# Decay and beta columns: the low parts of the weights beside the high ones in one weight tile

## The reference

```python
hn = rmsnorm(h, norm1)
proj = hn @ w_in                      # ga and gb are 8 columns each
beta = jax.nn.sigmoid(gb)
log_g = -jnp.exp(a_log) * jax.nn.softplus(ga + dt_bias)
o_a = gated_delta_chunked(gq, gk, gv, log_g, beta)
```

## Time and profile before

| | |
|---|---|
| median of three runs | 2068.93 us (2068.31 to 2069.67) |
| profiled execution | 2070.8 us |
| its span | 2069.0 us |
| TensorE busy | 2034.7 us (98%), 12940 matmul instructions |
| TensorE weight loads | 1949.7 us (94%) |
| VectorE busy | 1176.3 us (57%) |
| ScalarE busy | 626.6 us (30%) |
| GpSimd busy | 287.4 us (14%) |

### The profile page before, as it was taken

The page is one execution under the profiler, slowest core; times in us unless marked ns, Lnnn a source line. Parts: engine busy times, 40 slices in busy tenths (PEclk is TensorE's granted clock), DMA queues, the critical chain, the costliest instruction groups (busy, mean ns, idle before and its releaser), DMA issues.

```text
span 2069.0 us, 30409 instructions
## 1 busy us (share of the span) xinstructions
PE 2034.7 (98%) x12940; PEld 1949.7 (94%) x12940; DVE 1176.3 (57%) x1357; ACT 626.6 (30%) x794; POOL 287.4 (14%) x275
## 2 busy tenths in 40 slices
PE   8999999999999999999999999999999999999998
PEld 8999998999999999999999999999999999999996
DVE  6457565566667656566433343466565656565656
ACT  5223334434333444344443332211111111111113
POOL 0000003758370222222000002000000000000002
PEclk9999999999999999999999999999999999999999
DMA  9235666654555754645153221111011101110102
GB/s 281 93 103 136 142 158 202 187 191 154 163 154 133 173 177 137 187 146 156 60 186 109 88 70 51 62 61 52 31 51 51 52 31 51 52 53 31 60 31 82
DMA packets 252204, 227.11 MB, mean 110 GB/s; under 512 B 141102, under 2 KB 209622, under 8 KB 251942
## 3 DMA queue, kind: packets, MB, share of 16 engines
q1 hardware_dynamic: 252070, 225.17, 36.0%
HBM read 161.29 MB, written 63.84 MB: 109 GB/s over the span
## 4 chain that ended last, share of the span: by engine, by line
PE 91%; DVE 3%; ACT 2%; DMA 2%; issue 2%; SPq 1%; POOL 0%; POOLq 0%; DVEq 0%; ACTq 0%
PE a_psum L895 33%; PE a_psum L145 31%; PE a_psum L1164 11%; PE a_psum L882 5%; PE a_psum L970 1%; PE a_psum L988 1%; PE a_psum L1071 1%; PE a_psum L998 1%; PE a_psum L952 1%; PE a_psum L1014 1%; DMA w_raw<-in_w_in 1%; PE a_psum L967 1%; PE a_psum L1086 1%; PE a_psum L1094 1%; PE a_psum L1085 1%
## 5 line engine op out<-in xcount | busy, mean ns | idle before, releaser
L895 PE MATMUL a_psum<-xh,w_hi 128*128 128x342 f32 (+3 forms) x1656 | 535.6, 323 | 3.9 <-DVE w_lo L1515 3.9
L895 PE MATMUL a_psum<-xl,w_hi 128*128 128x342 f32 (+3 forms) x1656 | 531.4, 321 | 0.0
L895 PE MATMUL a_psum<-xh,w_lo 128*128 128x342 f32 (+3 forms) x1656 | 529.7, 320 | 0.0
L895 PEld LDWEIGHTS a_psum<-xh,w_hi 128*128 128x128 f32 x1656 | 312.2, 189 | 7.1 <-DVE w_lo L1515 4.5
L895 PEld LDWEIGHTS a_psum<-xl,w_hi 128*128 128x128 f32 x1656 | 312.3, 189 | 1.0
L895 PEld LDWEIGHTS a_psum<-xh,w_lo 128*128 128x128 f32 x1656 | 312.2, 189 | 0.0
L1218 ACT ACTIVATE w_hi<-w_raw 128x1024 fp32r<-128x1024 f32 x125 | 132.0, 1056 | 433.1 <-PE a_psum L145 409.5
L1293 ACT ACTIVATE post<-a_psum 128x342 f32<-128x342 f32 (+3 forms) x207 | 94.7, 457 | 554.2 <-PE a_psum L895 518.5
L145 PE MATMUL a_psum<-xh,w_hi 128*128 128x342 f32 (+1 forms) x1152 | 245.1, 321 | 9.2 <-DVE xl L1537 9.2
L1515 DVE TENSOR_TENSOR w_lo<-w_raw,w_hi 128x1024 fp32r<-128x1024 f32 x125 | 156.6, 1253 | 159.6 <-ACT w_hi L1218 159.6
L145 PE MATMUL a_psum<-xl,w_hi 128*128 128x342 f32 (+1 forms) x1152 | 245.1, 321 | 0.0
(11 more groups left out here) (239 smaller groups left out, 2807.8 us busy)
## 6 DMA issues: line engine op xcount, KB each, us to landing
w_raw<-in_w_in SPq DMA_DIRECT2D x76, 512.0 KB, 3.7
w_raw<-in_w_up SPq DMA_DIRECT2D x44, 512.0 KB, 3.5
mix_scratch<-post SPq DMA_DIRECT2D x32, 522.0 KB, 2.8
down_raw<-in_w_ffn_down SPq DMA_DIRECT2D x22, 512.0 KB, 4.3
ext<-mix_scratch SPq DMA_DIRECT2D x9, 1024.0 KB, 6.9
y<-mix_scratch SPq DMA_DIRECT2D x18, 512.0 KB, 5.5
ext<-grow_scratch SPq DMA_DIRECT2D x9, 512.0 KB, 5.5
ext<-mix_scratch SPq DMA_DIRECT2D x9, 512.0 KB, 6.8
```

The costliest lines, as they stand in the source:

```text
L895: mm = pe.matmul(psum[:, u % 2, 0:n], w[:, k, :], x[:, k, at0:at0 + n], start=(k == 0 and part == 0), stop=(k == KC - 1 and part == 2))
```

## The change

Tile 16 uses 16 of its 128 weight columns. After the change VectorE writes the low parts of these 16 columns not into the tile of low parts but into columns 16 to 31 of the tile of high parts. One product of x with the first 32 columns then gives both the high and the low weights' share, in rows 0 to 15 and 16 to 31 of PSUM. It is taken with x high and x low: 8 blocks x 2 x 3 thirds = 48 matmuls, with 32 weight columns each. (The share of low by low, which was left out before, is in it.) ScalarE copies 32 rows instead of 16 to `abT`. The turn is no longer nine transposes but nine ordinary float32 matmuls: `abT`'s 32 rows x 128 columns are the weights, and the moving operand is a new constant (`C_FOLD`) of 32 rows x 16 columns with ones where row modulo 16 is the column, so that a high and a low row are added as they are turned. The constants' table grows by 16 columns, which moves what lies behind it in SBUF by 64 bytes a partition.

```diff
+C_FOLD = C_BLK + 4
+C_W_ALL = C_FOLD + 2 * GH
...
+    c[:, C_FOLD:C_FOLD + 2 * GH] = i[:, None] % (2 * GH) == np.arange(2 * GH)[None, :]
...
-        abT = y[0:2 * GH, 0:2, :].rearrange("p k t -> p (k t)")[:, 0:TW]
+        abT = y[0:4 * GH, 0:2, :].rearrange("p k t -> p (k t)")[:, 0:TW]
...
                         if t == T_AB:
                             pe.wait_ge(x_split, KC + k + 1)
-                        mm = project_block(pe, psum, 2 + 3 * (t - T_AB + 1), wh[t % 2], wl[t % 2], xh, xl, k, 0, N3)
+                            for part, x in enumerate((xh, xl)):
+                                for j in range(3):
+                                    mm = pe.matmul(psum[0:4 * GH, 5 + j, 0:N3], wh[t % 2][:, k, 0:4 * GH],
+                                                   x[:, k, N3 * j:N3 * j + N3], start=(k == 0 and part == 0),
+                                                   stop=(k == KC - 1 and part == 1))
+                            continue
+                        mm = project_block(pe, psum, 2, wh[t % 2], wl[t % 2], xh, xl, k, 0, N3)
...
-                            mm = pe.transpose(psum[:, 7, c * 2 * GH:(c + 1) * 2 * GH],
-                                              abT[:, c * CH:c * CH + CH], ident[0:2 * GH, 0:2 * GH])
+                            mm = pe.matmul(psum[:, 7, c * 2 * GH:(c + 1) * 2 * GH], abT[:, c * CH:c * CH + CH],
+                                           const(C_FOLD, 2 * GH)[0:4 * GH, :], start=True, stop=True)
...
-                        act.activation(abT[:, LEAD:TW].rearrange("p (b c) -> p b c", b=3), psum[0:2 * GH, 5:8, 0:N3],
+                        act.activation(abT[:, LEAD:TW].rearrange("p (b c) -> p b c", b=3), psum[0:4 * GH, 5:8, 0:N3],
...
-                dve.tensor_tensor(lo, wr(t), hi.bitcast(F32), ALU.subtract).then_inc(w_lo, 1)
+                raw_w = wr(t)
+                if t == T_AB:
+                    n = 2 * GH
+                    hi, lo, raw_w = hi[:, :, 0:n], hi[:, :, n:2 * n], raw_w[:, :, 0:n]
+                dve.tensor_tensor(lo, raw_w, hi.bitcast(F32), ALU.subtract).then_inc(w_lo, 1)
```

More of the change, by code:

```diff
@@ L84 @@
 C_BLK = C_RCOL + RH
-C_W_ALL = C_BLK + 4
+C_FOLD = C_BLK + 4
+C_W_ALL = C_FOLD + 2 * GH
 RV_STEPS = ([(0, 512, (c,)) for c in range(9)]
```

## The result

The changed kernel took 2072.6 us, the median of 20 runs (2069.99 to 2077.08), beside 2069.77 us for the kernel before (20 runs, 2067.33 to 2072.71). The ratio is 1.0017, 95% interval 1.0012 to 1.0023, which is +3.5 us (+2.5 to +4.8) on 2069.77. The plain difference of the two medians is 2.8 us, inside that interval. In a second comparison on one chip the ratio was 1.0020 (1.0011 to 1.0028), +4.1 us. The forecast was +2.6, called no measurable change. The sign was right and the size lies at the lower edge of the interval, but the measurement told the change from none.

The account below looks back on a forecast made before the run. TensorE, busy for 98% of the span, was taken as the bound, with tile 17 held by VectorE's low parts. Terms -0.15 + 1.51 + 1.2 = +2.56 us on 2068.93 gave 2071.5 us, range 2068.7 to 2073.2.

Parts of the forecast that it names:

- The bound and the wait: TensorE bounds the kernel, but tile 17 waits for VectorE's low parts with 0.31 us slack; shortening tile 16's low part gains nothing.
- Term 1: Tile 16: 24 fewer products save 3.82 us, but TensorE then stalls 3.40 us ahead of tile 17; net -0.15 us.
- Term 2: After the stall ahead of tile 17 the granted clock falls to 0.50, as after the stall at 700.5; +1.51 us.
- (a): Ahead of tile 17: the stall comes but the clock stays; +1.05 us, 2070.0, chance 0.19.
- (d): From tile 17 on: the clock falls and stays low until after the turn; +5.9 us, 2074.8, chance 0.06.
- Term 3: The turn: nine transposes become 18 float32 instructions at 0.106 us each, 1.91 instead of 0.66 us; +1.2 us.
- The step from the sum to the chances: With 0.2% (4.1 us) as about what a measurement can tell: faster 0.01, same 0.93, slower 0.06.
- The range: Whole kernel: bounds of +0.3 and +3.6 us, with 0.7 for the medians' spread, given as 2068.7 to 2073.2 us.
- (b): Tile 16's shorter low part is passed on, tile 17's weights come 1.1 us sooner; -0.05 us, 2068.9, chance 0.06.
- (c): Tile 17's low parts are not last, so all 3.82 us of removed products count; -2.6 us, 2066.3, chance 0.04.

Follow-up runs that it names:

- e1: The changed kernel with tile 17's low parts and tile 18's weight load moved ahead of the last rotary step; -2.3 us against the kernel before (-4.1 to -0.4).
- e5: The kernel before with only the order changed: tile 17's low parts and tile 18's load ahead of the last rotary step; +0.2 us (-1.7 to 1.9).
- e2: The changed kernel with 12 unused filler products behind tile 16; 2071.96 us, +2.3 us against the kernel before (0.4 to 4.1).
- e7: The changed kernel in its own order, with nine 32-row transposes as the turn and VectorE adding the halves; +6.8 us against the kernel before (4.8 to 9.1).
- e0_after: The changed kernel unaltered, run and profiled again; 2074.61 us against 2069.56 for the kernel before, local measure +5.43 us.
- e3: The kernel before with all 72 products and only the turn changed, to nine float32 products of 16 rows; +2.1 us (0.2 to 3.9), local +1.43.
- e8: As e1, but tile 18's load stays behind the rotary stores in SyncE's queue; +0.4 us against the kernel before (-1.2 to 2.3).
- s1_fold: A second profile of e7, with no further change; local measure +2.72 us against the kernel before.
- s1_after: One more profile of the changed kernel, with no further change; local measure +4.35 us against the kernel before.

## Why the prediction was right in its mechanism and wrong in its size

- **The bound and the wait.** Right. Slack 0.31 us; the low parts of tile 17 did not move against tile 15, and the shortened instruction (0.29 us) became waiting. e1 and e5 show it from both sides: the same edit of the order (and of tile 18's load) is worth nothing before the change and turns the changed kernel's +4.1 to -2.3.
- **Term 1, -0.15 us.** Right: tile 17 starts 22.65 us after tile 15 instead of 22.91, and loses 0.11 in its first product. The stall was 3.49 us, forecast 3.40.
- **Term 2, the clock, +1.5 us.** This step failed in its size. I took the one example in the trace as the price. The cost is a distribution: 1.55, 4.13, 3.05 and 1.53 us in four profiles of the changed kernel (local difference minus the 1.30 of the other terms), mean 2.6. Two of the four agree with the 1.51 of the forecast; the other two have a low stretch of about twice the length or a second one, or both. Filling the stall (e2) took away 1.8 to 2.65 us of the time, which agrees with 2.6 and does not exclude 1.5. The mean local measure, +3.87, lies within the measured interval of +2.5 to +4.8.
- **Rivals (a) and (d).** (a), no fall behind the stall, did not occur in four profiles of the changed kernel; behind the same stall in e7 it occurred once in three. (d), a clock that stays low until after the turn, occurred in none: where the first stretch was long, as in e0_after, it ended ahead of the turn, and the turn took 2.11 us at full clock. What came instead was a fall behind the turn, which no rival named. The mistake was the same in all of them: each gave the clock one value for all executions, where it differs from one execution to the next. The single value of the likeliest draw lay 1.1 us below the mean.
- **Term 3, the turn, +1.2 us.** Right in mechanism, short by 0.25: 18 instructions in 2.11 us (0.117 each) instead of 1.91, and the late first instruction, which the forecast dropped, stayed (212.21 to 212.46). e3 measured +1.43. The kind of the load, not its rows, set the price (187 ns at 16 and at 32 rows, 136 for a transpose of 16); its columns, 128 in all of them, were not varied.
- **The step from the sum to the chances.** This failed too. I took 0.2% as the least that a measurement tells. Twenty runs of each kernel gave an interval of 0.12% to 0.23%. With +2.6 us (0.12%) forecast, no measurable change should not have held 0.93.
- **The range.** Its lower end is a slip: 2068.93 + 0.3 - 0.7 is 2068.5, not 2068.7. Nothing hangs on it.
- **The other rivals.** (b) and (c) did not occur. (c) was said to need another order on VectorE. e1 is that order, and its sum, -2.6, is what e1 measures locally, -2.48; but e8 shows that the order on VectorE alone is not enough, tile 18's load must move too.

## What to carry to other kernels

Before counting the products that an edit removes, look up how much slack the next wait had: what exceeds it (3.5 of 3.8 us here) turns into a stall. A stall of TensorE of this length is not merely a lost gain, for the clock may be low behind it, at 0 to 4 us from one execution to the next (2.2 us in the mean of the seven profiles here); so price it by a mean over several profiles, not by one example. Then move the work that is waited for, and with it everything that its followers need from other queues: here one instruction on VectorE and one load on SyncE's queue made the difference between +4 and -2 us.

## What the runs showed of the hardware

- The clock's fall is not a fixed consequence of a stall. A stall of 3.49 us was followed or accompanied by a low clock in six of seven profiles. The fall came anywhere from 1.1 us ahead of the first product behind the stall (s1_fold) to 1.2 us after it (s1_after), and the first low stretch took 1.5 us from TensorE in three of the six and 2.6 us in the other three.
- The length of the stall does not decide. One of 1.58 us (e2) had no low clock behind it, one of 2.36 us (e8) had one, and the wait of 1.28 us at 689.7 in the changed kernel, with sixteen products of 32 columns behind it, had one too; the same wait, 1.19 us long, had none in the kernel before.
- A fall need not cost what it takes: the changed kernel's low stretch at 692.2 was taken up by the next wait for low parts, which was 1.07 us long instead of 2.69.
- The clock can be low a second time with no stall ahead: twice in four profiles behind the stall of 3.49 us and the 18 products of 16 columns, never in the four kernels with the same 18 products behind a shorter stall or none.
- A float32 product of 16 moving columns costs 0.117 us per instruction with 128 weight columns, at 16 and at 32 rows alike, and a transpose 0.073 (16 rows, 16 columns) to 0.074 (32 rows, 32 columns). The product is two instructions, the transpose one.
- Weights of 32 instead of 128 columns did not shorten products of 348 columns: 48 took 7.56 us, 0.158 each, where 128-column ones took 0.159.
